# Row sums of squares of a differential attention's heads by a column of ones, and the head's last steps in another order

## The reference

```python
    for blk in range(s // Q_BLOCK):
        ...
        probs = jax.nn.softmax(scores + bias[None, :, None], axis=-1)
        weights = probs[:, :, 0] - lam * probs[:, :, 1]
        outs.append(jnp.einsum('bhqk,bkhe->bqhe', weights.astype(v.dtype), vb))
    o = jnp.concatenate(outs, axis=1)
    o = rms_norm(o, head_norm_g) * (1.0 - lam_0)
    o = o.reshape(b, s, BRANCH) * jax.nn.silu(z)
    return x + o @ w_out
```

## Time and profile before

| | us |
|---|---|
| median of 3 runs | 1295.86 |
| lowest, highest | 1295.49, 1296.67 |
| the profiled execution | 1295.79 |
| its span | 1294.1 |

### The profile page before, as it was taken

The page is one execution under the profiler, slowest core; times in us unless marked ns, Lnnn a source line. Parts: engine busy times, 40 slices in busy tenths (PEclk is TensorE's granted clock), DMA queues, the critical chain, the costliest instruction groups (busy, mean ns, idle before and its releaser), DMA issues.

```text
span 1294.1 us, 18343 instructions
## 1 busy us (share of the span) xinstructions
PE 1284.3 (99%) x7158; PEld 1081.6 (84%) x7158; DVE 795.4 (61%) x1577; ACT 611.4 (47%) x1300; POOL 304.8 (24%) x203
## 2 busy tenths in 40 slices
PE   8999999999999999999999999999999999999999
PEld 6777888888889999998888887887888888887787
DVE  5435665333479888887334647576767666677743
ACT  4336654333435444445234446555556555656531
POOL 2022310000055656640002402122222213131110
PEclk9999999999999999999999999999999999999999
DMA  7322232332633334243235222222222222223511
GB/s 233 106 57 74 58 98 66 98 98 98 208 118 102 102 124 129 68 131 114 82 111 214 98 85 78 66 74 82 82 98 74 73 74 74 75 73 124 184 60 66
DMA packets 110297, 130.35 MB, mean 101 GB/s; under 512 B 7553, under 2 KB 87425, under 8 KB 110210
## 3 DMA queue, kind: packets, MB, share of 16 engines
q1 hardware_dynamic: 104450, 112.39, 26.7%
q10 hardware_dynamic: 5760, 16.78, 3.5%
HBM read 119.72 MB, written 9.44 MB: 100 GB/s over the span
## 4 chain that ended last, share of the span: by engine, by line
PE 94%; DVE 4%; ACT 1%; issue 1%; DMA 0%; POOL 0%; SPq 0%; DVEq 0%; ACTq 0%
PE ps L865 17%; PE ps L867 16%; PE ps L866 16%; PE ps L870 7%; PE ps L872 6%; PE ps L871 6%; PE ps L1089 5%; PE ps L1092 5%; PE ps L1091 5%; PE ps L1147 3%; PE ps L1157 1%; DVE wlo L1527 1%; PE ps L1129 1%; PE ps L1181 1%; PE ps L1171 1%; PE ps L1172 1%
## 5 line engine op out<-in xcount | busy, mean ns | idle before, releaser
L1527 DVE TENSOR_TENSOR wlo<-raw,whi 128x512 fp32r<-128x512 f32 (+1 forms) x294 | 239.9, 842 | 173.7 <-ACT whi L1211 172.8
L1211 ACT ACTIVATE whi<-raw 128x512 fp32r<-128x512 f32 (+2 forms) x338 | 208.7, 650 | 115.9 <-PE ps L867 90.2
L865 PE MATMUL ps<-whi,hth 128*128 128x512 f32 x592 | 244.3, 413 | 0.2 <-DVE wlo L1527 0.2
L867 PE MATMUL ps<-wlo,hth 128*128 128x512 f32 x592 | 231.8, 392 | 0.0
L866 PE MATMUL ps<-whi,htl 128*128 128x512 f32 x592 | 231.2, 391 | 0.0
L1947 POOL TENSOR_TENSOR wlo<-raw,whi 128x384 fp32r<-128x384 f32 (+1 forms) x44 | 48.8, 1127 | 418.1 <-ACT whi L1211 418.1
L865 PEld LDWEIGHTS ps<-whi,hth 128*128 128x128 f32 x592 | 111.3, 188 | 31.3 <-issue 9.5
L867 PEld LDWEIGHTS ps<-wlo,hth 128*128 128x128 f32 x592 | 111.2, 188 | 25.0
L866 PEld LDWEIGHTS ps<-whi,htl 128*128 128x128 f32 x592 | 111.6, 189 | 18.9
L1477 ACT ACTIVATE px<-px,nm 128x128 f32<-128x128 f32 (+3 forms) x128 | 70.7, 554 | 90.3 <-DVE nm L1860 90.3
L870 PE MATMUL ps<-hth,whi 128*128 128x512 f32 (+1 forms) x288 | 111.9, 389 | 0.0
(11 more groups left out here) (347 smaller groups left out, 2858.5 us busy)
## 6 DMA issues: line engine op xcount, KB each, us to landing
raw<-in_l_w_in SPq DMA_DIRECT2D x64, 512.0 KB, 4.4
raw<-in_w_gate_up SPq DMA_DIRECT2D x44, 512.0 KB, 4.6
raw<-in_w_in SPq DMA_DIRECT2D x13, 1024.0 KB, 5.1
raw<-in_w_down SPq DMA_DIRECT2D x10, 1024.0 KB, 4.8
raw<-in_l_w_out SPq DMA_DIRECT2D x8, 1024.0 KB, 4.9
raw<-in_w_in SPq DMA_DIRECT2D x26, 256.0 KB, 3.4
raw<-in_w_branch SPq DMA_DIRECT2D x8, 512.0 KB, 3.8
raw<-in_w_out SPq DMA_DIRECT2D x4, 1024.0 KB, 4.8
```

Source lines behind the costliest of these rows:

```text
L865: e.matmul(o, ah, wh[:, cs], start=a, stop=False)
L867: m = e.matmul(o, ah, wl[:, cs], start=False, stop=z)
L1211: return e.activation(out, in_, ACT.Copy, **how)
L1527: return e.tensor_tensor(out, src, hi_part.bitcast(F32), ALU.subtract)
```

## The change

For heads 0 to 11 (`ROWS = 12`) the sums of squares are made the other way round. The ones are stationary (`ones_r`, one column, `fp32r`) and the squares are moved, 512 tokens at once, in two parts. This needs `osq` split: ACT makes `osh` in its part of `p2`; the new step `gl`, first in the slot, ahead of `s2 .. 0`, has DVE make the remainder `osl`. The new step `gr`, in the place of `ga` and with a bank of its own, has PE make the two matmuls into one partition of 512 sums, has ACT copy that row, scaled and with the four token blocks side by side, over `osq`'s first partition, and has ACT issue a DMA that spreads it to 128 partitions by 4 (`hn`). POOL waits for the landing and adds epsilon itself, ahead of the power. `gb` on DVE and `ga` on PE remain for heads 12 to 15.

For the same heads `to` moves from ahead of `t2 .. 2` to the slot's end, ahead of `p2`. `t2 .. 1` no longer shares its bank. `st` is made shorter and the scratch column of it moves.

```diff
--- before.py
+++ after.py
@@ -21,6 +21,7 @@
 MASKED = -1e37
 H1 = 8
 H2 = 16
+ROWS = 12
 LAM0 = 0.2
 QSEG = [0, 128, 384, 768]
 KSEG = [0, 512, 896, 1152]
@@ -499,7 +500,10 @@
     def slot(self, h):
         put = self.put
         now, last, out = h < H2, 1 <= h <= H2, 2 <= h
+        by_row = 2 <= h < ROWS + 2
         if now:
+            if by_row:
+                put("gl", h - 2)
             put("s2", h, 0, self.bank(), self.bank())
             yield
         if h == 1:
@@ -512,8 +516,10 @@
             if h + 1 < H2:
                 put("ab", h + 1)
         if last:
+            if by_row:
+                put("gr", h - 2, self.bank())
             b = self.bank()
-            if out:
+            if out and not by_row:
                 put("ga", h - 2, b, 3 * P)
             put("t2", h - 1, 1, b)
             if out:
@@ -534,6 +540,8 @@
             put("s2", h, 2, self.bank(), self.bank())
             put("cb", h, 2)
             yield
+        if by_row:
+            put("to", h - 2, self.bank())
         if last:
             put("p2", h - 1, self.bank())
         if now:
@@ -609,9 +617,10 @@
         tab = sbuf(ctx, "tab", [P, S])
         lam = sbuf(ctx, "lam", [P, 8])
         gh = sbuf(ctx, "gh", [P, 4])
-        st = sbuf(ctx, "st", [P, 64])
+        st = sbuf(ctx, "st", [P, 56])
         neghalf = sbuf(ctx, "neghalf", [P, 8])
         ones = sbuf(ctx, "ones", [P, 1])
+        ones_r = sbuf(ctx, "ones_r", [P, 1], F32R)
         raw = [sbuf(ctx, f"raw{i}", [P, 2048]) for i in range(3)]
         whi = [sbuf(ctx, f"whi{i}", [P, 2048], F32R) for i in range(2)]
         wlo = [sbuf(ctx, f"wlo{i}", [P, 2048], F32R) for i in range(2)]
@@ -681,6 +690,7 @@
         og = sbuf(att, "og", [P, TB, P])
         oc = sbuf(att, "oc", [P, S])
         osq = sbuf(att, "osq", [P, S])
+        osh, osl = (sbuf(att, n, [P, S], F32R) for n in ("osh", "osl"))
         v2h = [both(att, f"v2h{i}", [P, TB, 256]) for i in range(2)]
         v2l = [both(att, f"v2l{i}", [P, TB, 256]) for i in range(2)]
         zs = [sbuf(att, f"zs{i}", [P, TB, 256]) for i in range(2)]
@@ -693,6 +703,7 @@
         nm2, ls2, rl2 = (sbuf(att, n, [P, 16]) for n in ("nm2", "ls2", "rl2"))
         rq = sbuf(att, "rq", [P, 3, 8])
         hn = sbuf(att, "hn", [P, 8])
+        row = osq[0:1, :]
         att.close()
 
         special = {
@@ -772,6 +783,8 @@
                              "p2_pe", "oc_a"))
         ss_pe, hvar_d, hpow_p, og_p, to_pe, ot_d2, ot_hi, ot_lo, yo_d = (
             sem(n) for n in ("ss_pe", "hvar_d", "hpow_p", "og_p", "to_pe", "ot_d2", "ot_hi", "ot_lo", "yo_d"))
+        ones_rounded, osh_a, osl_d, row_a, hn_in, hvar_p = (
+            sem(n) for n in ("ones_rounded", "osh_a", "osl_d", "row_a", "hn_in", "hvar_p"))
 
         SMALL = 16 * 14
         QBS1 = [(0, 1), (2,), (3,)]
@@ -1157,7 +1170,7 @@
                         m = e.transpose(ps[b][:, P * c:P * c + P],
                                         px[2 * (h % 2)][:, QSEG[qb] + P * kb:QSEG[qb] + P * kb + P], ident[:])
                     m.then_inc(t2_pe, 1)
-                    free[b] = [(pt2_lo, 3 * h + i + 1)] + ([(hvar_d, h)] if i == 1 and h >= 1 else [])
+                    free[b] = [(pt2_lo, 3 * h + i + 1)] + ([(hvar_d, h - ROWS)] if i == 1 and h > ROWS else [])
                 elif kind == "p2":
                     h, b = a
                     g, vc = h // 2, slice(P * (h % 2), P * (h % 2) + P)
@@ -1172,6 +1185,15 @@
                         m = e.matmul(o, vhi, ptl2[:, ks], start=False, stop=kb == TB - 1)
                     m.then_inc(p2_pe, 1)
                     free[b] = [(oc_a, 2 * h + 2)]
+                elif kind == "gr":
+                    h, b = a
+                    claim(b)
+                    pe.wait_ge(osh_a, h + 1)
+                    pe.wait_ge(osl_d, h + 1)
+                    pe.wait_ge(ones_rounded, 1)
+                    e.matmul(ps[b][0:1, :], ones_r[:, 0:1], osh[:], start=True, stop=False)
+                    e.matmul(ps[b][0:1, :], ones_r[:, 0:1], osl[:], start=False, stop=True).then_inc(ss_pe, 1)
+                    free[b] = [(row_a, h + 1)]
                 elif kind == "ga":
                     h, b, c = a
                     claim(b)
@@ -1216,7 +1238,7 @@
                 e.dma_start(raw[0][:, 512 * kt:512 * kt + 512], kview(A["w_in"][0], kt, 1, C_V, 512)[:, 0, :]).then_inc(
                     raw_first[kt], 16)
             act.wait_ge(const, 1)
-            e.activation(st[:, 62:63], neghalf[:, 0:1], ACT.Exp).then_inc(warm_a, 1)
+            e.activation(st[:, 54:55], neghalf[:, 0:1], ACT.Exp).then_inc(warm_a, 1)
 
             for s in STEPS:
                 kind, a = s[0], s[1:]
@@ -1264,6 +1286,8 @@
                     copy(wf2[:, :, 0:H1], wfv).then_inc(wf_hi, 1)
                     act.wait_ge(ident_made, 1)
                     copy(id8[:], ident[:, 0:H1]).then_inc(id8_made, 1)
+                    act.wait_ge(ones_made, 1)
+                    copy(ones_r[:], ones[:]).then_inc(ones_rounded, 1)
                 elif kind == "qko":
                     which, j = a
                     act.wait_ge(mm, MM["qk", which, 1, j, 2])
@@ -1495,7 +1519,21 @@
                     act.wait_ge(to_pe, h)
                     act.wait_ge(ot_d2, h)
                     copy(oc[:], ps[b][:, :]).then_inc(oc_a, 1)
+                    act.wait_ge(osl_d, min(h, ROWS))
+                    act.wait_ge(hn_in, 16 * min(h, ROWS))
                     e.activation(osq[:], ps[b][:, :], ACT.Square).then_inc(oc_a, 1)
+                    if h < ROWS:
+                        act.wait_ge(oc_a, 2 * h + 2)
+                        act.wait_ge(ss_pe, h)
+                        copy(osh[:], osq[:]).then_inc(osh_a, 1)
+                elif kind == "gr":
+                    h, b = a
+                    act.wait_ge(ss_pe, h + 1)
+                    copy(row.rearrange("a (p q) -> a q p", q=TB), ps[b][0:1, :].rearrange("a (q p) -> a q p", p=P),
+                         scale=1.0 / P).then_inc(row_a, 1)
+                    act.wait_ge(row_a, h + 1)
+                    act.wait_ge(hpow_p, h)
+                    e.dma_start(hn[:, 0:4], row.rearrange("a (p q) -> a p q", q=TB)).then_inc(hn_in, 16)
                 elif kind == "to":
                     h, b = a
                     act.wait_ge(ot_d2, h + 1)
@@ -1880,10 +1918,16 @@
                     cs = slice(KSEG[i], KSEG[i] + n)
                     dve.wait_ge(pt2_hi, 3 * h + i + 1)
                     lower(ptl2[:, cs], ps[b][:, 0:n], pth2[:, cs]).then_inc(pt2_lo, 1)
-                elif kind == "gb":
+                elif kind == "gl":
+                    h, = a
+                    dve.wait_ge(osh_a, h + 1)
+                    dve.wait_ge(ss_pe, h)
+                    lower(osl[:], osq[:], osh[:]).then_inc(osl_d, 1)
+                elif kind == "gb" and a[0] >= ROWS:
                     h, b, c = a
                     dve.wait_ge(ss_pe, h + 1)
                     dve.wait_ge(to_pe, h)
+                    dve.wait_ge(hpow_p, h)
                     e.tensor_scalar(hn[:, 0:4], ps[b][:, c:c + 4], 1.0 / P, EPS, ALU.mult, ALU.add).then_inc(hvar_d, 1)
                 elif kind == "to":
                     h, b = a
@@ -2001,8 +2045,13 @@
                 elif kind == "gb":
                     h, b, c = a
                     rb = hn[:, 4:8].rearrange("p (a d) -> p a d", d=1).to_broadcast([P, TB, P])
-                    pool.wait_ge(hvar_d, h + 1)
                     pool.wait_ge(to_pe, h)
+                    if h < ROWS:
+                        pool.wait_ge(hn_in, 16 * h + 16)
+                        e.tensor_scalar(hn[:, 0:4], hn[:, 0:4], EPS, None, ALU.add).then_inc(hvar_p, 1)
+                        pool.wait_ge(hvar_p, h + 1)
+                    else:
+                        pool.wait_ge(hvar_d, h - ROWS + 1)
                     e.tensor_tensor(hn[:, 4:8], hn[:, 0:4], neghalf[:, 0:4], ALU.pow).then_inc(hpow_p, 1)
                     pool.wait_ge(hpow_p, h + 1)
                     pool.wait_ge(vz_d, 8 * (h // 2) + 8)
```

## The result

The changed kernel takes 1309.28 us (median; 1306.85 to 1310.76), the kernel before 1296.04 in the same comparison: a ratio of 1.0099, 95% interval 1.0087 to 1.0110. The forecast was 1301.8, slower by 0.44%, with a range up to 1308.5. It is slower, by 13.2 us and not by 5.9. The spans of the two profiled executions differ by 14.1.

A forecast was written before the change was run, and what follows sets the result against it. The prediction took TensorE (PE), busy 99% of 1294.1 us, as the bound. It summed -3.9 saved on PE, +7.0 odd-slot stalls and +2.8 in the last heads to +5.9 us: forecast 1301.8, range 1291.7 to 1308.5.

The forecast's parts named there:

- PE's saving: On PE, `gr` takes 0.46 us per head where `ga` took 0.80; net of the join of `to`, -3.9 us.
- The moved gate: Even slots: ACT's `oc` waits for `ots`, starting at 913.04 instead of 911.16; the probabilities' copy is 1.45 us late.
- The bank: Odd slots: `t2 .. 1` waits for `qkl` to free its bank; PE stands 1.0 us, with later stalls 7.0 in all.
- The even slots: POOL does `og` ahead of `qn`, bringing `qn` to 1.8 us later and `qs` some 0.15 later against PE.
- a landing over 2.5: Sign against the forecast: the row's DMA landing over 2.5 us after its issue, where 2.0 was taken.
- a hole at `qt 0` of an even slot: Sign against the forecast: PE standing at `qt 0` of an even slot, where no hole was forecast.
- rival (c): The row's DMA lands late, deciding from about 2.5 us; a landing at 3.6 gives near 1308.5; 0.18 with (d).
- The row copy: ACT's copy of one partition of 512 sums: bound 0.4 to 0.8 us, taken as 0.6, the duration of `oc`.
- the issue: ACT's issue of the row's DMA: 0.33 us, with ACT's next start 0.37 after the issue.
- the landing: The row's 2 KB DMA lands 2.0 us after its issue from ACT, with 1.6 and 5 kept as ends.
- (d): Rival: no saving on PE, each `gr` costing 0.8 us as `ga` did, 4.1 more, 1305.9; 0.18 with rival (c).
- The last heads: PE, 0.8 us late itself, stands 2.8 us before `to` of head 12, waiting for `og`.

The follow-up runs named there:

- e10: e9 without the remainder: squares of heads 0 to 11 rounded as written, one matmul in `gr`; 1289.84 us, ratio 0.9947 to the kernel before.
- e9: e6 with the gate's transposes of head 12 in the later place too; 1293.40 us, ratio 0.9978 to the kernel before.
- e11: Changed kernel with `gr` behind `t2 .. 1` instead of ahead of it, its bank taken one turn later; 1311.53 us.
- e2: Kernel before with only the gate's transposes moved to the head's end for heads 0 to 11; 1297.12 us, ratio 1.0005.
- e4: Changed kernel with squares written rounded at once: no `osh`, no `gl`, one matmul in `gr`; 1295.34 us.
- e3: Changed kernel without the row sums' DMA: POOL waits for the row copy and makes its four columns from a constant; 1299.11 us.
- e8: Changed kernel with the row of sums copied straight, without laying the four token blocks side by side; 1310.14 us.
- e1: Changed kernel with the remainder `gl` one place later, behind the first scores' maxima; 1302.01 us.
- e5: Changed kernel with the gate's transposes one place earlier, ahead of the third scores in place of the head's end; 1295.54 us.
- e12: Changed kernel with the gate's transposes back ahead of `t2 .. 2` for all heads, the sums as changed; 1300.36 us, ratio 1.0029.
- e6: Changed kernel with both the remainder behind the first scores and the gate ahead of the third; 1294.31 us, ratio 0.9986 to the kernel before.

## Why the prediction was right, and where it was wrong

What was measured is 7.3 us above the sum of the forecast (13.2 to 5.9). In the table that is 3.8 ahead of `qt 0`, 1.5 of PE's clock, 1.4 ahead of `p2`, 1.2 in three smaller places, less 0.5 in the holes that were forecast.

**PE's saving** was right: two matmuls at 0.23 where eight took 0.80, -3.9 us. e10 leaves out one of the two, and PE has the same two small holes as in e9: it has 553.4 us behind the first `qt` where e9 has 556.5, 3.1 less, and 12 x 0.23 is 2.8.

**The moved gate** was right in its mechanism and too small: ACT's `oc` behind `ots`, forecast 913.04, comes at 914.18, the probabilities' copy late by 2.6 against 913.25 of the earlier trace rows. PE itself runs some 0.7 later here, so 1.9 counts where 1.45 was forecast. DVE and ACT in the changed kernel, to be laid beside the earlier trace rows:

```profile
912.99 0.74 DVE L1940 SCALAR_TENSOR_TENSOR ots<-oc,gh,ps 128x512 f32<-128x512 f32 x1
...
916.58 0.75 DVE L1914 SCALAR_TENSOR_TENSOR px<-px,rl 128x512 f32<-128x512 f32 x1 [2.53 <-ACT px L1233]
...
919.06 0.68 DVE L1565 TENSOR_TENSOR osl<-osq,osh 128x512 fp32r<-128x512 f32 x1
...
923.12 0.88 DVE L1568 SCALAR_TENSOR_TENSOR qkl<-ps,gh,qkh 128x256 fp32r<-128x256 f32 x2
```

```profile
914.18 0.60 ACT L1233 ACTIVATE oc<-ps 128x512 f32<-128x512 f32 x1 [2.73 <-DVE ots L1940]
914.68 0.59 ACT L1524 ACTIVATE osq<-ps 128x512 f32<-128x512 f32 x1
915.30 0.63 ACT L1233 ACTIVATE osh<-osq 128x512 fp32r<-128x512 f32 x1
915.84 0.71 ACT L1233 ACTIVATE px<-px,rl 128x512 f32<-128x512 f32 x1
...
922.27 0.82 ACT L1233 ACTIVATE qkh<-ps,gh 128x256 fp32r<-128x256 f32 x2
...
926.65 1.05 ACT L1233 ACTIVATE osq<-ps 1x512 f32<-1x512 f32 x1
```

**The bank** was right in place, sign and size: DVE's `qkl` (923.12 to 924.00) frees the bank, PE starts at 924.05; 6.5 us in six holes, 7.0 forecast. e11 shows that it is the bank, e2 that without the extra turn and the sums' added work the late gate is covered, e4 that without `osh` and `gl` nearly all is. The size is in part luck: 0.47 of each hole is lag that came round through the DMA's way (e3), for which the forecast had 0.15, and the sum took 1.2 for a hole that its working made 1.15.

**The even slots** is the step that failed: "POOL does `og` ahead of `qn`, which brings `qn` to 1.8 later, and `qs` to some 0.15 later against PE". There are 3.8 us of holes where I had none, and the prediction had named both a landing over 2.5 and a hole at `qt 0` of an even slot as signs that it would be wrong. POOL and PE there:

```profile
897.96 0.23 POOL L2051 TENSOR_SCALAR hn<-hn 128x4 f32<-128x4 f32 x1 [16.76 <-DMA hn<-osq]
898.26 1.05 POOL L2055 TENSOR_TENSOR hn<-hn,neghalf 128x4 f32<-128x4 f32 x1
899.40 1.04 POOL L2058 TENSOR_TENSOR og<-zs,hn 128x512 f32<-128x512 f32 x1
900.39 1.64 POOL L1960 TENSOR_TENSOR rq<-rq,neghalf 128x8 f32<-128x8 f32 x1
```

```profile
902.22 0.39 PE L880 MATMUL ps<-wlo,hth 128*128 128x512 f32 x1
902.90 0.63 PE L1142 MATMUL ps<-ident,qn_f 128*128 128x128 f32 x4 [0.30 <-DVE qn_f L1868]
```

`og` ends at 900.44 and POOL's power for `qn` stands right behind it, at 900.39, 2.8 later than at the like place of the kernel before (897.62), where the forecast had 1.8; DVE's `qs` ends at 902.76, PE starts at 902.90, 0.45 late. So a lag 1.0 above the forecast's makes 0.45 of a hole: about half a us was spare here, and not the 1.1 of my rival (c). From the row copy's start to `og`'s end it takes 6.8 us where the forecast had 5.6. Three terms were too short, each taken from the nearest row of another operation. The row copy took

```profile
893.68 1.05 ACT L1233 ACTIVATE osq<-ps 1x512 f32<-1x512 f32 x1
894.76 0.48 ACTq L1536 DMA_DIRECT2D hn<-osq  x1
```

1.05 for 0.6; the issue 0.48 for 0.33, which counts for ACT alone, as the landing is measured from the issue's start; the landing 3.05 to 4.17 us in five of the six even slots for 2.0 (2.0 to 2.5 in the odd ones), right behind a weight load in flight (e8). The remainder's 0.6 in the even slots is no term of the prediction, and it wasn't covered (e1). Which of these one takes away matters little: the holes ahead of `qt 0` go with the remainder moved (e1), with the DMA left out (e3), and with the gate earlier (e5, e12). POOL's add (0.23 for 0.4) and `og` (1.04 for 1.31) gave 0.4 back. My rival (c) had this mechanism, at 0.18 together with (d), "from about 2.5 us"; it was the case. That its price for a landing at 3.6, 1308.5, is near what was measured is in part luck: its sum has 0.9 us that come from no row, and 1.6 more ahead of `to` of head 12, where only 0.4 more were found, and it has nothing for `p2` and for the clock.

**Ahead of `p2`** I had not looked: at the head's end `p2`'s bank is the one of the third scores' first maximum. By my numbers that was free 0.9 us ahead; it came 0.2 late in five even slots. The sixth hole, in the slot of head 13, isn't the bank's: there `p2` waits 0.5 us for its own operand, DVE's `ptl`.

**The last heads**: the hole ahead of `to` of head 12 was right in place and size, 3.2 for 2.8. What I had no term for comes behind it. PE's timeline there:

```profile
1207.86 0.39 PE L880 MATMUL ps<-wlo,hth 128*128 128x512 f32 x1
1211.28 1.09 PE L1210 MATMUL ps<-ident,og 128*128 128x128 f32 x4 [3.03 <-POOL og L2058]
...
1212.66 0.78 PE L878 MATMUL ps<-whi,hth 128*128 128x512 f32 x1
1213.23 0.63 PE L879 MATMUL ps<-whi,htl 128*128 128x512 f32 x1
1213.66 0.63 PE L880 MATMUL ps<-wlo,hth 128*128 128x512 f32 x1
1214.08 0.48 PE L878 MATMUL ps<-whi,hth 128*128 128x512 f32 x1
```

From 1212.66 on a 512-column matmul takes 0.57 and 0.43 to the next start, not 0.23, and is back to 0.32 and then 0.23 by 1214.40. The windows around it (us, then busy time and instructions of PE, its weight load, DVE, ACT and POOL, the granted clock, DMA share, GB/s) show why:

```profile
1200.00:1207.00 7.00, 7.00 (x40) 5.56 (x39) 5.44 (x17) 4.59 (x14) 0.00 (x0) 1.00 0.36 138
1212.00:1214.00 2.00, 2.00 (x8) 1.79 (x7) 1.55 (x3) 0.52 (x2) 0.00 (x0) 0.50 0.79 305
```

The clock was 1.00 before the hole and 0.50, 1.2 GHz, after it. PE had stood for 3.2 us. The same happens in the five other kernels with a hole of 3.2 us there (e1, e4, e8, e11, e12), and in none of the three in which it is 2.1 to 2.5 (e3, e5, e6). The Trainium skill (TensorE: Matmul & The Clock Gate, "HAM oscillation — how this bites in real kernels") describes idle time costing clock besides itself. The trace agrees: together with the transposes of `to` and `t2` behind the hole it comes to some 1.5 us.

**The range** was too narrow at the top by 0.8 us. I had sized the landing by the nearest row, a DMA that met no weight load, and the top of the range by 3.6 alone, though I had kept 5 as the late end of that term. And nothing in it stood for the remainder of the even slots, the bank of `p2` or the clock.

## What to carry to other kernels

When PE has no wait left, the question of a change isn't what it saves on PE but which covered wait it uncovers: count for each bank turn who freed it last, and lay the margin beside the lag that the new steps bring. A step that takes a buffer turn of its own moves every later step of the rotation to another predecessor. The small DMA issued behind a large load landed with the load here, so its price is to be read from what is in flight, not from another DMA's median. PE's hole of 3.2 us cost it some 1.5 us of clock besides. And the same edit in another order turned a loss of 1.0% into a gain of 0.2% (e9, 1293.4).

## What the runs showed of the hardware

- A copy of one partition with 512 values out of PSUM takes 0.57 us straight and 1.05 when written with a stride of four values (e8). I had not thought that the stride would matter at one partition.
- ACT's issue of the DMA that spreads 2 KB over 128 partitions takes 0.48 us, that of a 256 KB store 0.33.
- Such a DMA landed 2.0 to 4.2 us after its issue, in 11 of 12 slots of the changed kernel 0.15 to 0.4 us after the load of 512 KB or 1 MB that was in flight. None went out without a load in flight.
- After 3.2 us in which PE stood, the granted clock was 0.50 from 1210.9 to 1214.3, and the matmuls' pace about halved; in e11 it stayed down twice as long. After holes of 2.1 to 2.5 us it stayed at 1.00 (e3, e5, e6).
- POOL's multiply of 128x512 (`og`) took 1.31 to 1.37 us in the pair of the earlier trace rows and 1.04 in all heads of the changed kernel. The difference goes with DVE's subtraction for a weight (`wlo`, two inputs from SBUF): over all runs 34 of the 224 multiplies took more than 1.1 us, 1.13 to 1.49, and every one of them overlaps a `wlo`; the 175 that overlap none took 1.04. In the even slots of the kernel before the `wlo` is stretched too, 1.53 for 0.69. No run varies this alone.
- The one landing of 4.17 us, 1.25 after its load, stays open.
